# Attention levels copied under masks, pooling set between weight slots, norm statistics kept on VectorE

## Chip, cores and metric

The kernel runs on one core of one Trainium2 chip. The metric is the device time of one execution in microseconds. Before the change it is 1908.38 us (median of 3 runs, 1907.46 to 1908.57).

## What is computed

Two blocks on 256 tokens of width 2048, all in float32. Block one has two layers of sliding-window and latent attention and isn't touched. Block two has an even layer (gated linear attention beside a convolution) and an odd layer (pooling), each with a modulation and a layer norm. Cut to what the change touches:

```
# even layer, one head of 4, 256 wide, 256 tokens, forward and backward:
#   o_i = sum_j (q_i * exp(g_i - g_j)) . k_j v_j  + state term, g = cumulative log gate
# odd layer
h = (x * (1 + sc) + sh) @ w_in_o                  # 256 x 4096
xp, gate = split(h, 2)                            # 2048 each
for g, window in enumerate((2, 4, 8, 16)):        # 512 columns each, window over grid rows
    z_g = window_mean(xp_g) - xp_g
    z_g = z_g @ w_pool[g]                         # 512 x 512
y = (z * pool_scale * silu(gate)) @ w_out_o       # 2048 x 2048
# behind each layer
x = layer_norm(alpha * x + gt * y, ln_g, ln_b)    # mean and variance over 2048
```

## The kernel before

**Weight stream.** All large products run over a stream of 504 slots. A slot is a 128 x 1024 piece of weights (512 KB). SyncE loads it into a ring of four stages; ScalarE rounds it to the high part `wh` (L257, `split_hi`); VectorE subtracts to get the low part `wl` (L278, `split_lo`); TensorE does 12 products of 128x512 with it (L325 to L327) and then frees one of four split buffers (`split_free`). Eight slots make a group, that is 512 output columns, in one of two PSUM banks `L[0]`, `L[1]`; an evacuation frees the bank (`psum_free`). The input `xth`/`xtl` of a product is made by transposes (L404, two PSUM banks `TP`), rounded by ScalarE (L424) and subtracted by VectorE (L430). Every engine runs its own list in order; semaphores by name tie them. Between slots VectorE also sums up the modulation (`mod_next`, L569).

**Gated attention.** For each of four heads, pairs of tokens are treated in levels of block size b = 1, 2, ... 64, then 128 between the two halves, then the state term (level index v = 0 to 8). In a level ScalarE takes four exponentials (L881) of prefix and suffix sums, VectorE scales queries and keys with them (L1394, L1395), TensorE forms the products (L1936) into `AB[0]` or `AB[1]` in turn and then does one weight slot, and VectorE updates the sums for the next level (L1400 to L1403; the pair L1400/L1401 feeds the keys' side, L1402/L1403 the queries'), splits one slot (L278) and adds the previous level's products to the score matrix: `masked(v - 1)` multiplies the bank with the level's 0/1 mask into `LT` (L1385), waits, and adds `LT` to `ATd` (L1386); for level 7 it copies the bank to `ATo` (L1388). The masks of the levels don't overlap. At the head's end TensorE multiplies `ATd`, `ATo` and the states with the values (L1950 to L1954) into `AB[0]`. Ahead of the levels stand the head's transposes, its gate product (L1917), ScalarE's log-sigmoid (L905 to L908), VectorE's gate (L1363) and two fills with zeros (L1365, L1366).

**Odd layer.** 64 slots (`R_ODD`, eight groups: four of `xp`, four of `gate`), written as a first group with transposes, one group, and a loop over three pairs. ScalarE copies each group to `Z` or `gate`. Then TensorE does the four pooling sums (L1997), each waiting for VectorE's L1537 (`pooled`) of the one before, while ScalarE applies silu to all of `gate` (L1010). Then 8 pooling slots (`pool_step`) with transposes of `Z` between; `evac_pool` scales the result into `Z` (L1546) and multiplies with the gate (L1549). When all four are done (`y_done`), the transposes of `Z` and the 32 output slots follow, with the modulation of the gate rows (L1800) behind the first group, and `evac_residual` adds each group to `X` (L1481, L1486). ScalarE issues three row loads (L960) for that before it.

**Layer norm.** After the last residual ScalarE sums `X` (L975) and squares the deviations (L979), two passes of 2048 each; VectorE turns the sums into mean and variance (L1493, L490), ScalarE takes the root (L485, with a table load), VectorE the reciprocal and `nmr` (L493, L1496), ScalarE scales `X` (L987), VectorE applies gain and shift (L1505, L1506).

Of the kernel before, what the change touches and what calls it, by code (L numbers as in the profile page):

```python
# [19 lines left out]
P = 128  # L20
# [94 lines left out]
def build(nc, A, out):  # L115
    ctx = ExitStack()
    with ctx:
# [33 lines left out]
        st = sb("st", [P, 64])  # L151

# [94 lines left out]
        LT = pa[:, 1024:1280].rearrange("p (j i) -> p j i", j=TT)  # L247
# [352 lines left out]
        def _(act):  # L600
# [295 lines left out]
            for hd in range(GH):  # L896
# [16 lines left out]
                for v, b in enumerate(LEVELS + [128]):  # L913
                    k = 9 * hd + v
                    act.wait_ge(once("sums_ready"), k + 1)
                    if k:
                        act.wait_ge(once("qk_scaled"), k)
# [5 lines left out]
                    if (hd, v) in EVAC:  # L923
# [9 lines left out]
                                     AB[0][:, :].rearrange("p (t n) -> p t n", t=TT), ACT.Copy)\  # L933
# [36 lines left out]
            def layer_norm_act(k, e):  # L970

                act.wait_ge(psum_free, (G_BLOCK1 + R_KV + R_EVEN + R_OUT + k * (R_ODD + 4 + R_OUT)) + 2)
                junk = [ar(0, D), ar(6144, D)]
                for t in range(TT):
                    ins = nc.scalar.activation(junk[t], X[:, t, :], ACT.Copy, accum_out=ss[:, t:t + 1])  # L975
                ins.then_inc(once("ln_sum"), 1)
                act.wait_ge(once("ln_mu"), k + 1)
                for t in range(TT):
                    ins = nc.scalar.activation(junk[t], X[:, t, :], ACT.Square, bias=nmu[:, t:t + 1],  # L979
                                               accum_out=ss[:, t:t + 1])  # L980
                ins.then_inc(st_sum, 1)
                stats_act_root(act, rstd, e)
                act.wait_ge(once("ln_nmr"), k + 1)
                for c in range(4):
# [3 lines left out]
                    ins.then_inc(once("ln_scaled"), 1)  # L988

# [17 lines left out]
            split_pairs(act, split_hi, R_ODD0, 2, evac_to(0, 1024, 2048), turn=turn_odd)  # L1007
            split_pairs(act, split_hi, R_ODD0 + 4, 2, evac_to(4096, 1024, 2048))
            act.wait_ge(psum_free, G_BLOCK1 + R_KV + R_EVEN + R_OUT + R_ODD + 2)
            nc.scalar.activation(ar(4096, 4096), ar(4096, 4096), ACT.Silu).then_inc(once("gate_silu"), 1)  # L1010
            turn_and_split(act, split_hi, R_POOL0, turn_plain)
            act.wait_ge(once("y_done"), 2)
# [3 lines left out]
            split_pairs(act, split_hi, R_OUTO0, R_OUT // 2, None, final=True, turn=turn_plain)  # L1016
# [4 lines left out]
        def _(dve):  # L1021
# [330 lines left out]
            for hd in range(GH):  # L1352
# [6 lines left out]

                for d, dst in ((0, PF), (1, SB_)):  # L1360
# [180 lines left out]
            def evac_pool(g):  # L1541
# [8 lines left out]
                if g == 3:  # L1550
                    ins.then_inc(once("y_done"), 1)
# [12 lines left out]
            def turn_y1(m):  # L1564
                turn_plain(m)
                if m == SLOTS + 1:
                    gate_rows(1)
# [555 lines left out]
```

## Time and profile before

| | us |
|---|---|
| median of 3 runs | 1908.38 |
| the profiled execution's own time | 1907.66 |
| its span, first to last instruction | 1905.9 |
| TensorE products busy | 1771.0 (93%) |
| VectorE busy | 1333.5 (70%) |
| ScalarE busy | 939.7 (49%) |
| mean granted TensorE clock, share of full | 0.962 |

Busy time of products includes their overlap once. The span is what the profile shows; the time of an execution is 1.8 us longer here. A row of a timeline gives start and duration; an operation's duration may overlap the start of the next on the same engine by some 0.08 us, so steps are read from start to start. What stands in brackets is how long the engine was idle before and who released it. "issue" as releaser means that the profile shows none.

### The profile page before, as it was taken

The numbers are of one execution on the slowest core, as the hardware profiler recorded it, in microseconds if no ns is written. First come the engines' busy times: TensorE is split into PE (matmuls) and PEld (weight loads), VectorE is DVE, ScalarE is ACT, GpSimd is POOL, SyncE is SP. The second block draws the span as 40 slices with busy tenths as digits, with TensorE's granted clock in tenths as the row PEclk, the third lists the DMA queues.
The fourth block names the chain that finished last, engine by engine and source line by source line (L and its number), as shares of the span: only waits on it lengthen the run. The fifth ranks groups of instructions, "written<-read, shape, count | busy, mean of one in ns | idle before, by whom it ended". The sixth has DMA issues, their size and how long they took to land.

```text
span 1905.9 us, 22383 instructions
## 1 busy us (share of the span) xinstructions
PE 1771.0 (93%) x8116; PEld 1418.8 (74%) x8116; DVE 1333.5 (70%) x1777; ACT 939.7 (49%) x1389; POOL 139.2 (7%) x197
## 2 busy tenths in 40 slices
PE   6999999999999999999899989998989969998894
PEld 5887777878877778788577877776767758885683
DVE  4967777768677777678466688776876966664554
ACT  5546553455465634546554446555433374443334
POOL 1100000001000000011111100000100201110000
PEclk9999999999999999999799999999989979999997
DMA  8855444558654446689577733334965948882551
GB/s 274 289 195 188 164 152 154 177 173 284 216 187 155 156 149 231 214 314 321 177 230 247 275 113 119 116 111 142 333 253 189 349 162 285 290 290 86 188 179 64
DMA packets 107011, 390.30 MB, mean 205 GB/s; under 512 B 12407, under 2 KB 13183, under 8 KB 105215
## 3 DMA queue, kind: packets, MB, share of 16 engines
q1 hardware_dynamic: 75040, 268.99, 40.4%
q0 software_dynamic: 27648, 100.68, 16.9%
q10 hardware_dynamic: 4224, 19.31, 2.7%
q8 instruction: 62, 1.02, 0.2%
q14 instruction: 37, 0.30, 0.1%
HBM read 384.74 MB, written 4.19 MB: 204 GB/s over the span
## 4 chain that ended last, share of the span: by engine, by line
PE 79%; DVE 11%; ACT 4%; issue 3%; DMA 2%; ACTq 0%; SPq 0%; DVEq 0%
PE L L325 22%; PE L L327 21%; PE L L326 21%; PE TP L404 3%; DVE wl L278 2%; PE AB L1663 1%; DMA mstage<-in_w_mod 1%; PE AB L1592 1%; PE AB L1668 1%; PE AB L1997 1%; PE TP L1677 1%; PE AB L1667 1%; PE AB L1882 1%; PE AB L1954 1%; ACT wh L257 1%
## 5 line engine op out<-in xcount | busy, mean ns | idle before, releaser
L278 DVE TENSOR_TENSOR wl<-stage,wh 128x1024 fp32r<-128x1024 f32 x504 | 614.0, 1222 | 301.0 <-ACT wh L257 299.7
L325 PE MATMUL L<-wh,xth 128*128 128x512 f32 x1952 | 800.9, 410 | 11.2 <-issue 8.3
L257 ACT ACTIVATE wh<-stage 128x1024 fp32r<-128x1024 f32 x504 | 531.2, 1056 | 526.0 <-PE L L327 452.6
L327 PE MATMUL L<-wh,xtl 128*128 128x512 f32 x1952 | 774.6, 397 | 0.0
L326 PE MATMUL L<-wl,xth 128*128 128x512 f32 x1952 | 773.8, 396 | 0.0
L325 PEld LDWEIGHTS L<-wh,xth 128*128 128x128 f32 x1952 | 375.3, 192 | 104.2 <-issue 26.3
L327 PEld LDWEIGHTS L<-wh,xtl 128*128 128x128 f32 x1952 | 374.1, 192 | 82.3
L326 PEld LDWEIGHTS L<-wl,xth 128*128 128x128 f32 x1952 | 375.0, 192 | 76.5 <-issue 3.4
L569 DVE SCALAR_TENSOR_TENSOR macc<-mstage,scols,macc 128x1024 f32<-128x1024 f32 x240 | 307.1, 1279 | 11.4 <-DMA mstage<-in_w_mod 10.7
L593 POOL DMA_DIRECT2D mstage<-in_w_mod x192 | 138.8, 723 | 1568.0 <-DVE macc L569 966.0
L881 ACT ACTIVATE arena<-arena 128x256 f32<-128x256 f32 (+1 forms) x136 | 48.2, 425 | 63.9 <-DVE arena L1403 63.9
L679 ACT ACTIVATE pa<-TP 128x384 f32<-128x384 f32 x48 | 23.6, 491 | 105.7 <-PE TP L1677 105.7
L1103 DVE SCALAR_TENSOR_TENSOR pa<-tab,AB 128x384 f32<-128x384 f32 x48 | 26.6, 554 | 67.6 <-PE AB L1663 36.8
L667 ACT ACTIVATE pa<-pa,st 128x128 f32<-128x128 f32 x96 | 43.0, 450 | 56.1 <-DVE st L1112 36.4
L404 PE MATMUL TP<-ident,arena 128*128 128x128 f32 x344 | 52.9, 287 | 17.1 <-DVE xtl L430 7.6
L404 PEld LDWEIGHTS TP<-ident,arena 128*128 128x128 f32 x344 | 43.2, 149 | 28.3 <-issue 9.7
L404 PE MATMUL TP<-ident,X 128*128 128x128 f32 x144 | 24.5, 302 | 36.1 <-DVE X L1506 16.0
L404 PEld LDWEIGHTS TP<-ident,X 128*128 128x128 f32 x144 | 19.7, 156 | 40.4 <-issue 21.0
L424 ACT ACTIVATE xth<-TP 128x512 fp32r<-128x512 f32 x40 | 23.4, 590 | 52.3 <-PE TP L404 52.3
L643 ACT ACTIVATE arena<-L,st 128x512 f32<-128x512 f32 x60 | 37.8, 682 | 9.2 <-PE L L327 4.9
L430 DVE TENSOR_TENSOR xtl<-TP,xth 128x512 fp32r<-128x512 f32 x40 | 27.3, 686 | 14.5 <-ACT xth L424 14.5
L430 DVE TENSOR_TENSOR xtl<-pa,xth 128x512 fp32r<-128x512 f32 x40 | 27.6, 689 | 7.7 <-ACT xth L424 7.7
(184 smaller groups left out, 1380.8 us busy)
## 6 DMA issues: line engine op xcount, KB each, us to landing
stage<-in_w_stream SPq DMA_DIRECT2D x504, 512.0 KB, 4.4
mstage<-in_w_mod POOLq DMA_DIRECT2D x192, 512.0 KB, 6.3
X<-in_x SPq DMA_DIRECT2D x4, 512.0 KB, 8.5
arena<-in_ctx ACTq DMA_DIRECT2D x1, 2048.0 KB, 15.1
x_kept<-X ACTq DMA_DIRECT2D x1, 2048.0 KB, 10.1
X<-x_kept ACTq DMA_DIRECT2D x1, 2048.0 KB, 8.3
arena<-in_b_ada ACTq DMA_DIRECT2D x2, 1024.0 KB, 9.1
arena<-in_ln_b ACTq DMA_DIRECT2D x2, 1024.0 KB, 12.7
```

Of the source, the lines that this page charges most:

```text
L257: nc.scalar.activation(wh[:, s % SPLITS].rearrange("p a b -> p (a b)"), stage[:, s % RING, :], ACT.Copy).then_inc(hi_ready, 1)
L278: nc.vector.tensor_tensor(wl[:, s % SPLITS].rearrange("p a b -> p (a b)"), stage[:, s % RING, :], wh[:, s % SPLITS].rearrange("p a b -> p ...
L325: nc.tensor.matmul(o, xh, w[0], start=start, stop=False, skip_group_check=True)
L326: nc.tensor.matmul(o, xh, w[1], start=False, stop=False, skip_group_check=True)
L327: last = nc.tensor.matmul(o, xl, w[0], start=False, stop=True, skip_group_check=True)
L404: last = nc.tensor.transpose(bank[0:width, j, t * P:t * P + P], src(t), ident[:])
L430: nc.vector.tensor_tensor(lo, src[:, 0:n, :], hi.bitcast(F32), ALU.subtract).then_inc(bank_free(m), 1)
L569: nc.vector.scalar_tensor_tensor(out=acc, in0=block, scalar=col, in1=acc, op0=ALU.mult, op1=ALU.add).then_inc(mod_sum, 1)
L593: pool.dma_start(mstage[:, unit % MOD_UNITS, :].rearrange("p (c n) -> p c n", c=2), WM[n // KPB, :, 2 * cp:2 * cp + 2, COLS * k:COLS * k + ...
L643: ins = nc.scalar.activation(dst(t), L[bank][:, t, :], fn, scale=scale(t))
L667: ins = nc.scalar.activation(pr[b][:, a:a + w], pr[b][:, a:a + w], ACT.Exp, bias=ngm[:, 2 * b + t:2 * b + t + 1], scale=1.0 if swa else ML ...
L881: return nc.scalar.activation(dst, src, ACT.Exp, scale=1.0 / 16)
```

## The change

Four edits, all in block two:

1. `masked(v)` for levels 0 to 6 becomes one predicated copy of the product's bank into `ATd` under the level's mask, read as integers; `LT` goes. The last level (b = 128) leaves out L1400 and L1401 and the wait behind them. The final product waits for `ATo` only ahead of its last member, which moves behind the state products, and goes to `AB[1]`.
2. The two fills with zeros are issued ahead of the gate (L1363) and signal `sums_ready` there; ScalarE waits for the gate by itself in level 0.
3. The layer norm's mean and variance come from VectorE: `evac_residual` takes partial statistics (`bn_stats`) of each 512 columns, `layer_norm_dve` aggregates them; ScalarE's four passes go. `psum_free` is signalled with the first of the two residual additions.
4. In the odd layer every engine's list is written out slot by slot. ScalarE evacuates `gate` with silu directly. The pooling sums stand behind slots 33, 41, 49 and 53 of the 64, the transposes of `Z` behind the eight slots of the last group, and the transposes of the gated product behind pooling slots 3, 5, 7 and output slot 1; `y_done` is counted by group. The row loads wait for the last group.

```diff
-                        link(nc.vector.tensor_tensor(LT, bank, mk, ALU.mult))
-                        nc.vector.tensor_tensor(ATd, ATd, LT, ALU.add).then_inc(added, 1)
+                        nc.vector.copy_predicated(ATd, mk.to_broadcast([P, TT, P]), bank).then_inc(added, 1)
...
-                        nc.vector.tensor_tensor(sf[:, :, 0, :], sf[:, :, 0, :], pf[:, :, 1, b - 1:b].to_broadcast(shape), ALU.add)
-                        link(nc.vector.tensor_tensor(pb[:, :, 1, :], pb[:, :, 1, :], sb_[:, :, 0, 0:1].to_broadcast(shape), ALU.add))
+                        if b < P:
+                            nc.vector.tensor_tensor(sf[:, :, 0, :], sf[:, :, 0, :], pf[:, :, 1, b - 1:b].to_broadcast(shape), ALU.add)
+                            link(nc.vector.tensor_tensor(pb[:, :, 1, :], pb[:, :, 1, :], sb_[:, :, 0, 0:1].to_broadcast(shape), ALU.add))
...
+                nc.vector.memset(SF, 0.0)
+                nc.vector.memset(PB_, 0.0).then_inc(once("sums_ready"), 1)
                 for d, dst in ((0, PF), (1, SB_)):
...
-                nc.vector.memset(SF, 0.0)
-                nc.vector.memset(PB_, 0.0).then_inc(once("sums_ready"), 1)
...
-                pe.wait_ge(once("at_added"), k + 1)
+                pe.wait_ge(once("at_added"), k)
...
+                    if t == 0:
+                        pe.wait_ge(once("at_added"), k + 1)
+                    last = nc.tensor.matmul(o, ATo[:, 1 - t, :], Vf[:, 1 - t, vs], start=False, stop=True)
...
+                        if t == 0:
+                            ins.then_inc(psum_free, 1)
+                    link(ins)
+                    for t in range(TT):
+                        ins = nc.vector.bn_stats(parts[:, t, 2 * i + b, :], X[:, t, at(1024 * i + 512 * b, 512)])
+                    ins.then_inc(once("ln_parts"), 1)
...
             def layer_norm_dve(k, e):
+                dve.wait_ge(once("ln_parts"), 4 * k + 4)
+                for t in range(TT):
+                    ins = nc.vector.bn_aggr(moments[:, t, :], parts[:, t].rearrange("p g s -> p (g s)"))
+                link(ins)
+                mean, var = moments[:, :, 0], moments[:, :, 1]
+                nc.vector.tensor_scalar(rstd, var, 1.0, LN_EPS, ALU.mult, ALU.add).then_inc(st_ms, 1)
+                dve.wait_ge(st_sd, e + 1)
+                nc.vector.reciprocal(rstd, rstd).then_inc(st_rs, 1)
...
# ScalarE, odd layer
+            for n in range(4, 68):
+                if n < 10:
+                    turn_odd(n - 2)
+                hi()
+                if n >= 60:
+                    turn_plain(n - 60)
+                if n % 8 == 3 and n > 8:
+                    g = (n - 11) // 8
+                    slots_done(act, ODD + n - 3)
+                    for t in range(TT):
+                        dst = (Z if g < 4 else gate)[:, t, COLS * (g % 4):COLS * (g % 4) + COLS]
+                        ins = nc.scalar.activation(dst, L[g % 2][:, t, :], ACT.Copy if g < 4 else ACT.Silu)
+                    ins.then_inc(psum_free, 1)
+            hi(4)
+            for i in range(4):
+                if i:
+                    hi(2)
+                for m in range(2 * i, 2 * i + 2):
+                    turn_plain(m)
+            act.wait_ge(once("y_done"), 5)
...
# VectorE, odd layer
+            for n in range(4, 68):
+                if n < 10:
+                    turn_x1(n - 2)
+                lo()
+                mod_some(96, n - 4)
+                if n in (38, 46, 54, 58):
+                    pooled((38, 46, 54, 58).index(n))
+                if n >= 60:
+                    turn_plain(n - 60)
+            lo(2)
+            evac_pool(0)
+            lo(2)
+            evac_pool(1)
+            for i in range(4):
+                if i:
+                    lo(2)
+                if i in (1, 2):
+                    evac_pool(i + 1)
+                for m in range(2 * i, 2 * i + 2):
+                    turn_plain(m)
+            lo(5)
+            gate_rows(1)
...
# TensorE, odd layer
+            for n in range(SLOTS, 8 * SLOTS):
+                g, m = n // SLOTS, n % SLOTS
+                slot(pe, 8 * R_ODD0 + n, G + g, KPB * m, m == 0)
+                if n in (33, 41, 49, 53):
+                    pool_sums((33, 41, 49, 53).index(n))
+                if g == 7:
+                    pe.wait_ge(once("pooled"), m // 2 + 1)
+                    uses.append(turn_z(m))
...
+            for m in range(SLOTS):
+                turned(pe, uses[m])
+                slot(pe, 8 * R_POOL0 + m, G + R_ODD + m // 2, KPB * m, m % 2 == 0)
+                if m in (3, 5, 7):
+                    turn_y((m - 3) // 2)
+            for n in range(4 * SLOTS):
+                g, m = n // SLOTS, n % SLOTS
+                if n == 2:
+                    turn_y(3)
+                if g == 0:
+                    turned(pe, ys[m])
+                slot(pe, 8 * R_OUTO0 + n, G + R_ODD + 4 + g, KPB * m, m == 0)
+                if n == 7:
+                    modulation_gate(1)
```

## Rows read from the trace of the kernel before

**Rows 1.** Part 4 of the page: the chain that ended last, by engine.

```profile
PE 79%; DVE 11%; ACT 4%; issue 3%; DMA 2%; ACTq 0%; SPq 0%; DVEq 0%
```

**Rows 2.** Timeline of ScalarE, last slots (start, us, operation, [idle before]).

```profile
1865.14 1.06 ACT L257 ACTIVATE wh<-stage 128x1024 fp32r<-128x1024 f32 x1 [1.66 <-PE L L327]
1867.86 1.06 ACT L257 ACTIVATE wh<-stage 128x1024 fp32r<-128x1024 f32 x1 [1.66 <-PE L L327]
```

**Rows 3.** Busy time by stretch: one head, start of the pooling.

```profile
core 0: us, PE busy (x) PEld busy (x) DVE busy (x) ACT busy (x) POOL busy (x), PEclk, DMA share, GB/s
1145.43:1201.53 56.10, 51.09 (x258) 41.28 (x257) 45.57 (x85) 30.99 (x55) 0.00 (x0) 1.00 0.34 114
1719.00:1749.00 30.00, 21.99 (x63) 10.86 (x63) 10.78 (x15) 9.67 (x9) 0.00 (x0) 0.94 0.17 56
```

**Rows 4.** Timeline of VectorE, second head: level 1's start, level 6.

```profile
1162.11 0.69 DVE L1394 TENSOR_TENSOR pa<-arena 128x512 f32<-128x512 f32 x1 [0.44 <-ACT arena L881]
...
1185.11 0.68 DVE L1394 TENSOR_TENSOR arena<-arena 128x512 f32<-128x512 f32 x1
...
1186.31 0.42 DVE L1400 TENSOR_TENSOR arena<-arena 128x256 f32<-128x256 f32 x1
...
1187.44 0.42 DVE L1403 TENSOR_TENSOR arena<-arena 128x256 f32<-128x256 f32 x1
1187.78 1.22 DVE L278 TENSOR_TENSOR wl<-stage,wh 128x1024 fp32r<-128x1024 f32 x1
1188.91 0.42 DVE L1385 TENSOR_TENSOR pa<-AB,tab 128x256 f32<-128x256 f32 x1
...
1189.71 0.69 DVE L1394 TENSOR_TENSOR pa<-arena 128x512 f32<-128x512 f32 x1
```

**Rows 5.** Timeline of ScalarE there: exponentials of levels 1, 7 and 8.

```profile
1160.57 1.44 ACT L881 ACTIVATE arena<-arena 128x256 f32<-128x256 f32 x4 [1.22 <-DVE arena L1403]
...
1187.90 1.34 ACT L881 ACTIVATE arena<-arena 128x256 f32<-128x256 f32 x4 [2.31 <-DVE arena L1403]
...
1192.50 1.15 ACT L881 ACTIVATE arena<-arena 128x512 f32<-128x512 f32 x2 [2.31 <-DVE arena L1403]
```

**Rows 6.** Timeline of TensorE there: level 7, slot's last product, values.

```profile
1191.05 1.16 PE L1936 MATMUL AB<-pa 128*128 128x128 f32 x8 [0.68 <-DVE pa L1395]
...
1194.57 0.39 PE L327 MATMUL L<-wh,xtl 128*128 128x512 f32 x1
...
1196.08 0.67 PE L1950 MATMUL AB<-X,tail 128*128 128x256 f32 x2 [1.12 <-DVE tail L1388]
```

**Rows 7.** Timeline of VectorE around the first layer norm.

```profile
1523.02 1.29 DVE L1486 SCALAR_TENSOR_TENSOR X<-X,pa 128x512 f32<-128x512 f32 x2
...
1532.58 0.17 DVE L490 TENSOR_SCALAR st<-st 128x2 f32<-128x2 f32 x1 [4.14 <-ACT arena L979]
```

**Rows 8.** Timeline of ScalarE around the first layer norm.

```profile
1532.57 1.28 ACT L485 ACT_TABLE_LOAD   x1
...
1534.49 0.81 ACT L987 ACTIVATE X<-X,st 128x512 f32<-128x512 f32 x1 [0.43 <-DVE st L1496]
```

**Rows 9.** Groups of VectorE by line, first 900 us: the reduction.

```profile
L1107 DVE TENSOR_REDUCE st<-pa 128x1 f32<-128x256 f32 x48 | 19.6, 409 | 0.0
```

**Rows 10.** Timeline of TensorE from the last gate slot to the modulation.

```profile
1721.77 0.39 PE L327 MATMUL L<-wh,xtl 128*128 128x512 f32 x1
...
1797.61 0.60 PE L404 MATMUL TP<-ident,arena 128*128 128x128 f32 x4
...
1800.82 0.60 PE L404 MATMUL TP<-ident,arena 128*128 128x128 f32 x4
...
1809.45 3.00 PE L1800 MATMUL AB<-macc,ones 128*128 128x512 f32 x6
```

**Rows 11.** Timeline of TensorE, convolution's shifts: two sites, three slots between.

```profile
1366.93 1.88 PE L1971 MATMUL AB<-X,tab 128*128 128x512 f32 x4
...
1376.86 1.88 PE L1971 MATMUL AB<-X,tab 128*128 128x512 f32 x4
```

**Rows 12.** The row loads of L960 (six DMAs): time to landing.

```profile
DMA to landing us min/median/max: 6.5/9.8/14.3
```

More of the change, by code:

```diff
@@ L988, in layer_norm_act @@
                     ins.then_inc(once("ln_scaled"), 1)
+            Z, gate = ar(0, TT, D), ar(4096, TT, D)
             def turn_y(m):
@@ L1005, in turn_odd @@
                 turn_modulated(m, 2)
[L1007 to L1012, printed above, removed]
+            hi.n = 8 * R_ODD0 + 4
+            ODD, POOL, OUTO = 8 * R_ODD0, 8 * R_POOL0, 8 * R_OUTO0
+            for m in range(2):
+                turn_odd(m)
+            for n in range(4, 68):
[18 more added lines that the diff above has]
+            act.wait_ge(once("y_done"), 5)
             row_load(1, "b_ada", 4096)
@@ L1015, in _ @@
             row_load(1, "ln_b", 8192)
-            split_pairs(act, split_hi, R_OUTO0, R_OUT // 2, None, final=True, turn=turn_plain)
+            hi(OUTO + 4 * SLOTS - hi.n)
             layer_norm_act(1, 2 * DEPTH + 3)
@@ L1528, in turn_x1, with pooled @@
                 turn_scaled(m)
-            split_pairs(dve, split_lo, R_ODD0, 2, None, turn=turn_x1, beside=lambda i, n: mod_some(96 + 8 * i, n))
-            split_pairs(dve, split_lo, R_ODD0 + 4, 2, None, beside=lambda i, n: mod_some(112 + 8 * i, n))
+            lo.n = 8 * R_ODD0 + 4
             Z, gate = ar(0, TT, D), ar(4096, TT, D)
-            for g in range(4):
+            GO = G_BLOCK1 + R_KV + R_EVEN + R_OUT
+            def pooled(g):
                 dve.wait_ge(once("pool_sums"), g + 1)
@@ L1999, in _, with turn_z, turn_y @@
                 last.then_inc(once("pool_sums"), 1)
-            def pool_step(m):
-                g = m // 2
-                if m % 2 == 0:
-                    pe.wait_ge(psum_free, G + R_ODD + g + 1)
-                pe.wait_ge(lo_ready, 8 * R_POOL0 + m + 1)
-                for k in range(KPB):
-                    last = products(L[g % 2], m % SPLITS, k, KPB * m + k, m % 2 == 0 and k == 0)
-                last.then_inc(split_free, 1)
-            xt_pe(pe, u, Z, pool_step, lambda m: pe.wait_ge(once("pooled"), m // 2 + 1))
-            pe.wait_ge(once("y_done"), 2)
-            product_pairs(pe, R_OUTO0, G + R_ODD + 4, 2, turn=xt_group(pe, u, Z, R_OUTO0, G + R_ODD + 4),
-                          after=lambda: modulation_gate(1))
+            def turn_z(m):
+                transposes(pe, u, [lambda t, kt=2 * m + j: Z[:, t, kt * P:kt * P + P] for j in range(2)])
+                return u.n
+            xt_group(pe, u, X, R_ODD0, G, lambda m: pe.wait_ge(once("ln_done"), m // 2 + 1))()
+            uses = []
+            for n in range(SLOTS, 8 * SLOTS):
[6 more added lines that the diff above has]
+                    uses.append(turn_z(m))
+            ys = []
+            def turn_y(i):
+                pe.wait_ge(once("y_done"), i + 2)
+                for m in range(2 * i, 2 * i + 2):
+                    ys.append(turn_z(m))
+            for m in range(SLOTS):
[7 more added lines that the diff above has]
+                    turn_y(3)
+                if g == 0:
+                    turned(pe, ys[m])
+                slot(pe, 8 * R_OUTO0 + n, G + R_ODD + 4 + g, KPB * m, m == 0)
+                if n == 7:
+                    modulation_gate(1)
 def tables():
```

77 lines of the change are left out of this document (29 added, 48 removed).

## The prediction

> **What bounds the kernel now.** I read the chain of waits first. Four fifths of it are TensorE, a tenth VectorE [rows 1]: the kernel is a stream of 504 weight slots, and wherever the stream runs alone a slot costs TensorE 2.72 us (two splits by ScalarE, each released by the last product of a slot, lie 1867.86 - 1865.14 apart) [rows 2]. An edit off that path is worth nothing, so I looked for the stretches in which TensorE does not run slots back to back, with the view of busy time by stretch, and then at the timelines of the engines there. The change touches three such places. (a) The four heads of the gated attention: TensorE is busy 51.1 of 56.1 us of a head, and VectorE 45.6 [rows 3]. (b) The pooling: TensorE is busy 22 of 30 us from 1719, and much of that is pooling sums and not slots. (c) Two layer norms, in which TensorE stands still.
>
> **Part 1, levels under masks (four heads).** The reader is to see in VectorE's timeline that it has no idle time in a level: from one scaling (L1394) to the next are 4.60 us (1185.11 to 1189.71), of which the masked product and the addition (L1385, L1386) take 0.80 (1188.91 to 1189.71), the split L278 1.13, and the scalings and prefix sums 2.67 [rows 4]. The change makes one predicated copy of the two operations and of the wait between them. The trace has no predicated copy. The nearest row is L1400, an operation on 256 elements like it, 0.42 us; back to back such an operation costs 0.34 (L1403 to L278). I take 0.34, because one input comes from PSUM and one is the mask, as in L1385. The least is 0.2 (the 0.42 less what a start overlaps); the most I put at 0.61, a second pass over its 256 elements: L1394 with 512 elements takes 0.26 more than L1400 with 256.
>
> VectorE alone would then need 4.60 - 0.80 + 0.34 = 4.14. But another wait is close behind. The exponentials of the next level wait for the prefix sums and the next scaling for them: L1403 ends 2.75 after the first scaling (1187.86 - 1185.11), ScalarE starts 0.04 later and takes 1.34 [rows 4, 5]. In level 0, where nothing is masked, the scaling starts 0.10 after the exponentials' end (1160.57 + 1.44 = 1162.01, scaling at 1162.11, after 0.44 of idle time). So the level becomes 2.75 + 0.04 + 1.34 + 0.10 = 4.23 and the gain is 0.37, not 0.46. Any copy under 0.43 gives the same. TensorE needs about 3.7 us for a level: its products start at 1191.05 and the last product of the slot behind them is issued at 1194.57 and 0.23 long [rows 6], so it isn't the bound. Six of the intervals of a head (level 1 to 2 up to 6 to 7) gain it: 2.2 us.
>
> The last level drops two sums and the wait between them. Three steps take 1.13 (L1400 at 1186.31 to L1403 at 1187.44), and the one that stays 0.34, so 0.79 go [rows 4]; its exponentials are two, 1.15 us [rows 5]. VectorE would be 0.46 + 0.79 = 1.25 earlier at the final scaling, and the product with the values no longer waits for the copy L1388, but only for the scaling. Here TensorE itself is late next: level 7's products start 1.34 after the scaling of that level, its slot ends at about 1194.78, that is 3.73 later, so the values can start 5.07 after it instead of 6.37 (1196.08 - 1189.71) [rows 4, 6]. That is worth 1.3, not the 1.25 + 0.4 that the two edits promise apart. A head gains 2.2 + 1.3 = 3.5, four heads **14.0 us**.
>
> Zeros ahead of the gate: two fills leave the place between the gate's logarithm and the splits. ScalarE reaches the exponentials of level 0 only after its own second split of the head and a table load, so I count nothing (bounds -0.2 and +0.2 a head, that is the two sides of one operation of 256 elements).
>
> **Part 2, norm statistics (twice).** Before, after the last residual (L1486, ends 1523.02 + 1.29 = 1524.31) ScalarE makes two passes of copies and two of squares, loads a table at 1532.57 for 1.28, and starts to scale at 1534.49: 10.18 us [rows 7, 8]. After, VectorE has kept partial statistics at each of the four evacuations, and only those of the last lie on the path. For a statistic over 512 elements the nearest row is the reduction of 256, 0.409 [rows 9]; with the 0.26 for 256 more it is 0.67, 0.6 back to back. Chain: wait 0.04, two statistics 1.28, column update, two aggregations (tiny, like L490's 0.17) with their waits 0.45, epsilon 0.2; the table load starts (1532.57) before L490, the tiny operation that feeds the root, does (1532.58), so the wait doesn't hold it and it slides under the last slots; root, reciprocal and the product take what they take now, 0.64 (1533.85 to 1534.49). Sum 2.6; gain 10.18 - 2.6 = **7.6 us**, twice 15.2. Bounds of one statistic: 0.3 (half of what the reduction's row gives) to 1.2 (two passes), so 0.6 more to 1.2 less gain a norm; if the load is held by the wait, 1.3 is lost a norm. The six other pairs of statistics (1.3 us each) lie beside slots, where VectorE has a split of 1.13 and at most one multiply-add of similar length in 2.72; the split buffer is four deep, so a delay of 1.3 is not seen by TensorE. If that cover failed, it would be 6 x 1.3 = 7.8.
>
> **Part 3, pooling between slots.** Before, from the last slot's last product (1721.77 + 0.23 = 1722.0) to the start of the gate's modulation (L1800, 1809.45) are 87.4 us [rows 10]. In it: the pooling sums in a row with VectorE after each, a 4096-wide activation, 8 pooling slots, the wait for the last gated product, 8 output slots. After, the same TensorE work without the waits:
> - four groups of sums of four 128x512 products each, set between slots of the second half. Two such products (L1971) between slots stretch three slots from 8.16 to 9.93 (1366.93 to 1376.86) [rows 11], so 1.77 for two, 3.54 for four, 14.2 in all;
> - 8 transposes of Z behind slots: a slot with one takes 3.21 (1797.61 to 1800.82) [rows 10], 0.49 more, 3.9 in all;
> - 8 pooling and 8 output slots, 16 x 2.72 = 43.5;
> - 8 transposes of the gated product, 3.9 at the same price (they come in pairs and should cost a little less).
> Sum 65.5; gain 87.4 - 65.5 = **21.9 us**.
>
> Whether the waits go, I worked out slot by slot with these durations, counted from the first pooling slot. The pooled rows have slots between: sums 0 behind slot 33, VectorE takes them behind split 38, and sums 1 come behind slot 41. The third pooling bank needs VectorE's first evacuation (two operations of 512, one of 1024: 1.3 and 1.13 us, as in rows 4) by 10.9 + 0.85 us; it has read the bank at 9.1. The gated products end at 10.3, 15.8, 22.1, 28.5, and TensorE asks at 10.9, 17.2, 23.5, 29.8. Transposes of a pair also need the two banks of the pair before, freed at about 17.0, 23.4 and 29.8: nothing to spare. I count no stall, with 0 to 3 us in the range. The three rows for the final norm are issued at about 33 and needed at 47; such rows take up to 14.3 us to land [rows 12], so this too is just in time. No DMA is moved ahead of the weight queue. The activation goes into the evacuations from PSUM, and its table load under a slot. The loops over three pairs of groups are written out; as the slots of block one, also written out, I price that at nothing.
>
> **Sum.** 14.0 + 15.2 + 21.9 = 51.1. The profiled execution took 1907.66 (span 1905.9), so 1856.6; the median shown, 1908.38, is 0.7 above it: 1857.3, and I predict 1857.
>
> A page that speaks against part 1: the Trainium skill, VectorE: DVE Perf Modes, section "First, the fixed hardware budget", has two read ports a lane as the ceiling for the tensors that an instruction reads in a cycle. A predicated copy that fetched its old destination too would read three. By that rule the time would be that of rival 1 without the statistics, 1861; by L1385's row, where two inputs run in one pass, it is the forecast [rows 4]. The trace of before has no instruction with three.
>
> **Rivals.**
> 1. *Second pass.* Predicated copy at 0.61: the level is VectorE's, 3.80 + 0.61 = 4.41, gain 0.19 in six intervals, 1.3 at the end as before: 2.4 a head, 9.8 in all, 4.2 less. Statistics at 1.2 take another 1.2 x 2. 1857 + 6.6 = 1863.6. For: beside mask and new values the old ones have to stay, which may be done by reading them. Against: L1385 does as much with its operands in one pass. 0.13.
> 2. *The pooling's waits move instead of going.* VectorE is late with a gated product or with banks, or the rows land late and hold the modulation; the slack was zero in three places, and where TensorE waits for some us, as it does for each sum now, its clock falls too (granted 0.94 from 1719 to 1749) [rows 3]. The middle is a third of the gain, 7: 1864, up to 1872. For: the zero slack. Against: ScalarE and VectorE have only 1.1 and 1.7 us of work for a slot. 0.10.
> 3. *Slower than before.* The predicated copy as an operation that goes element by element, with 28 of them in VectorE's loop and everything behind them late. Norms, pooling, the dropped sums (4 x 0.79) and the freed copy L1388 (4 x 0.4) bring 41.9, so it decides from 41.9 / 28 = 1.5 us above the present 0.80, at 2.3 us a copy; at 3 us it is 28 x 2.2 - 41.9 = 20 slower, 1928. Nothing in the rows is near that (0.42 for 256 elements of any kind). 0.02.
> 4. *The heads don't gain*, since their end is set by another wait and what a level saves returns as a wait there: 1857 + 9 = 1866. Against: VectorE has no idle time in a level. 0.03.
>
> **Numbers.** Forecast 1857 with 0.72 (its own spread 1854 to 1860). The range 1853 to 1865 adds rival 1 and half of rival 2. What this measurement can tell from no change is about 0.2%, 4 us; all but rival 3 lie far beyond it: faster 0.97, same 0.01, slower 0.02.
>
> **What would show it.** Scalings 4.23 apart in levels 1 to 6, with VectorE idle 0.1 before them and ScalarE's exponentials as releaser; the predicated copy 0.42; first product with the values 5.1 behind level 7's scaling; ScalarE's scaling 2.6 behind the last residual, no table load between; slots 2.72 or 3.21 apart from the gates to the modulation, sums 3.5 between them, full clock throughout. Wrong it would be, if TensorE's timeline has gaps over 1 us there, or if a table load stands behind the statistics.

## Result and profile after

| | before | after |
|---|---|---|
| median, us (range, executions) | 1907.92 (1902.51 to 1908.57, 4) | 1851.46 (1847.59 to 1855.12, 4) |
| ratio of the executions | | 0.971, interval 0.9682 to 0.9738 |
| profiled execution, its own time / span | 1907.66 / 1905.9 | 1855.12 / 1853.3 |
| mean granted TensorE clock | 0.962 | 0.969 |

The kernel is 2.9% faster. The four executions before are the three named above and one beside the changed kernel (1902.51). The profiled execution lies 1.5 us from the 1856.6 of the prediction's sum; the median of the four, 1851.46, lies below its range (1853 to 1865). Both have to be explained, and they are two different things.

Page, part 4, the chain that ended last, by engine [rows 1]:

```profile
PE 81%; DVE 10%; ACT 4%; issue 2%; DMA 1%; SPq 0%; ACTq 0%; DVEq 0%
```

Timeline of VectorE in the second head, the scalings of levels 5 to 8 and the copies before them [rows 4]; L1398 is the predicated copy, L1406 the scaling:

```profile
1173.00 0.44 DVE L1398 COPY_PREDICATED tail<-tab,AB 128x256 f32<-128x256 uint32 x1
1173.43 0.69 DVE L1406 TENSOR_TENSOR pa<-arena 128x512 f32<-128x512 f32 x1
...
1177.24 0.44 DVE L1398 COPY_PREDICATED tail<-tab,AB 128x256 f32<-128x256 uint32 x1
1177.67 0.69 DVE L1406 TENSOR_TENSOR arena<-arena 128x512 f32<-128x512 f32 x1
...
1181.91 0.69 DVE L1406 TENSOR_TENSOR pa<-arena 128x512 f32<-128x512 f32 x1
...
1184.92 0.44 DVE L1398 COPY_PREDICATED tail<-tab,AB 128x256 f32<-128x256 uint32 x1
1185.25 0.68 DVE L1406 TENSOR_TENSOR arena<-arena 128x512 f32<-128x512 f32 x1
```

Timeline of ScalarE there, the exponentials [rows 5], and of TensorE, level 7 and the values [rows 6]:

```profile
1176.23 1.34 ACT L882 ACTIVATE arena<-arena 128x256 f32<-128x256 f32 x4 [1.95 <-DVE arena L1416]
```

```profile
1183.26 1.16 PE L1976 MATMUL AB<-pa 128*128 128x128 f32 x8 [0.32 <-DVE pa L1407]
...
1187.02 0.59 PE L1990 MATMUL AB<-X,tail 128*128 128x256 f32 x2
```

The scalings are 4.24 apart (1181.91 - 1177.67), 4.60 before. The step from the copy to the scaling is 0.43 where the exponentials end late (1176.23 + 1.34 = 1177.57), and 0.33 at the end of the head (1184.92 to 1185.25), where they are done: that is the copy's own step. The values start 5.11 behind level 7's scaling, 6.37 before, and TensorE no longer waits for them.

Timelines of VectorE, then of ScalarE, around the first norm [rows 7, 8]:

```profile
1506.42 1.22 DVE L279 TENSOR_TENSOR wl<-stage,wh 128x1024 fp32r<-128x1024 f32 x1
1507.56 1.28 DVE L1494 TENSOR_TENSOR pa<-L,arena 128x512 f32<-128x512 f32 x2
1508.87 1.29 DVE L1499 SCALAR_TENSOR_TENSOR X<-X,pa 128x512 f32<-128x512 f32 x2
1510.20 1.29 DVE L1505 BATCH_NORM_STATS2 parts<-X 128x6 f32<-128x512 f32 x2
...
1511.52 0.39 DVE L1512 BATCH_NORM_AGGREGATE moments<-parts 128x2 f32<-128x24 f32 x2
1511.94 0.17 DVE L1515 TENSOR_SCALAR st<-moments 128x2 f32<-128x2 f32 x1
```

```profile
1503.32 1.06 ACT L258 ACTIVATE wh<-stage 128x1024 fp32r<-128x1024 f32 x1 [0.76 <-PE L L328]
1504.39 1.28 ACT L486 ACT_TABLE_LOAD   x1
1512.14 0.20 ACT L486 ACTIVATE st<-st 128x2 f32<-128x2 f32 x1 [6.47 <-DVE st L1515]
1512.78 0.81 ACT L980 ACTIVATE X<-X,st 128x512 f32<-128x512 f32 x1 [0.43 <-DVE st L1519]
```

From the end of the last residual (1508.87 + 1.29 = 1510.16) to the scaling are 2.62 us, 10.18 before. The table load is issued ahead of the wait for the statistics, directly behind the last split.

Busy time by stretch (columns as in [rows 3]): one head, and the last 68.6 us up to the gate rows' modulation:

```profile
1139.93:1192.50 52.57, 50.70 (x258) 41.47 (x257) 42.55 (x76) 30.98 (x56) 0.00 (x0) 1.00 0.36 122
1696.00:1764.60 68.60, 68.60 (x333) 57.06 (x332) 51.68 (x55) 31.82 (x40) 0.72 (x1) 1.00 0.65 231
```

In the second row TensorE is busy for 68.60 of 68.60 us at full clock; in the kernel before it was busy 22 of 30 at the start of the pooling. Not one of the old waits has come back.

To say where the time went, I cut each trace at five points that every kernel has: the first product of a head with the values, the modulation of the gate rows, the start of the last residual group, ScalarE's first scaling of the norm, and again the gate rows. Differences of starts in us (heads: the mean period; even output: gate rows to last residual; odd: scaling to gate rows):

| | head | even output | residual to scaling | odd | last output | its residual to scaling |
|---|---|---|---|---|---|---|
| before | 56.10 | 71.51 | 12.79 | 274.96 | 69.23 | 12.80 |
| after | 52.59 | 73.52 | 5.22 | 251.70 | 69.22 | 5.23 |

The span is 52.5 us shorter. Of this, four heads bring 14.0, the odd layer 23.3 and the norms 15.1; the even output groups give back 2.0, and 2.0 come from ahead of the first line that differs. That adds up to 52.4.

### The profile page after: what moved, and what is told of

Same layout as the page of the kernel before. It is cut to its first block, busy times and chain, and to the rows that moved or that the text cites. A ratio compares the mean times of both kernels' runs of the same rounds, so it can differ in the third digit from the quotient of the medians.

```text
span 1853.3 us, 22300 instructions
## 1 busy us (share of the span) xinstructions
PE 1761.7 (95%) x8116; PEld 1415.7 (76%) x8116; DVE 1329.8 (72%) x1759; ACT 919.4 (50%) x1372; POOL 139.2 (8%) x197
## 4 chain that ended last, share of the span: by engine, by line
PE 81%; DVE 10%; ACT 4%; issue 2%; DMA 1%; SPq 0%; ACTq 0%; DVEq 0%
PE L L326 22%; PE L L328 22%; PE L L327 22%; PE TP L405 3%; DVE wl L279 2%; PE AB L1703 1%; PE AB L1632 1%; DMA stage<-in_w_stream 1%; PE AB L1708 1%; DVE macc L570 1%; PE TP L1717 1%; PE AB L1707 1%; ACT wh L258 1%; PE AB L1993 1%; PE AB L1922 1%
## 5 line engine op out<-in xcount | busy, mean ns | idle before, releaser
L431 DVE TENSOR_TENSOR xtl<-TP,xth 128x512 fp32r<-128x512 f32 x40 | 27.0, 685 | 10.4 <-ACT xth L425 10.4
L431 DVE TENSOR_TENSOR xtl<-pa,xth 128x512 fp32r<-128x512 f32 x40 | 27.6, 689 | 7.5 <-ACT xth L425 7.5
```

The costliest lines, as they stand in the source:

```text
L431: nc.vector.tensor_tensor(lo, src[:, 0:n, :], hi.bitcast(F32), ALU.subtract).then_inc(bank_free(m), 1)
```

## Experiments

**The changed kernel again, and each part alone.** The first run is the changed kernel unedited; the others are the kernel before with edits 1 and 2, with edit 3, and with edit 4.

> The changed kernel once more, the same code. The traces of before and after differ by 52.55 us of span, of which 1.97 lie ahead of the first line that the change touches, and the four executions of after spread over 7.5 us. Theory A (the terms were right, 51 to 52 us, and what moved the median out of the range is a spread of the whole program that has nothing to do with the change): against the kernel before on the same chip the gain is 50.5 to 52.5 us in the median, both kernels spread by several us, and the profile shows a different granted clock in stretches of block one. Theory B (the change gains more than its terms, 55 to 57 us, and the profiled execution was an unlucky one): gain 54 to 58 us, spread only in block two.

> Only the levels: predicated copy, dropped sums, freed last copy, fills ahead of the gate. By my terms 14.0 us less than before (3.5 a head, the level 4.24 us from scaling to scaling). Rival (the level was only paced by VectorE's 0.46 us): 18 us. Rival (something behind the heads gives it back): under 10 us.

> Only the norm statistics on VectorE. By my terms 15.2 us less than before, 7.6 a norm. In the trace of after the groups ahead of the first norm took 2.0 us longer than before; if the statistics between slots cause that (VectorE late with the modulation, so its loads are late), this kernel shows it too and gains 13 us, with TensorE waiting over 3 us for the last multiply-add of the modulation. If it is only how fast the loads came in that execution, it gains 15 us and the wait is as before, 1.3 us.

> Only the pooling between slots. By my terms 21.9 us less than before; the trace of after gives 23.0 between the first norm and the modulation, so 22 to 23. Rival (it needs the norm's shorter gap to come out so): 20 or less. No gap of TensorE over 1 us from the first gate group to the modulation.

| | median (range, executions) | ratio, interval | head | even output | residual to scaling | odd |
|---|---|---|---|---|---|---|
| again | 1854.70 (1848.91 to 1857.94, 5) | 0.9743, 0.9724 to 0.9761 | 52.56 | 73.17 | 5.22 | 251.88 |
| edits 1, 2 | 1890.62 (1888.35 to 1895.20, 6) | 0.9937, 0.9920 to 0.9953 | 52.58 | 72.10 | 12.79 | 274.55 |
| edit 3 | 1893.85 (1885.19 to 1897.25, 7) | 0.9954, 0.9935 to 0.9973 | 56.12 | 73.79 | 5.22 | 274.19 |
| edit 4 | 1879.00 (1877.24 to 1885.92, 4) | 0.9872, 0.9854 to 0.9890 | 56.11 | 71.82 | 12.79 | 252.18 |

The kernel before had 1902.67 beside them (1899.56 to 1908.24, 12). The heads are moved by edits 1 and 2 alone, the odd stretch by edit 4, the way from the residual to the scaling by edit 3, each by as much as in the changed kernel, so the stretches show no exchange between the parts. One column gets worse, the even output, and only where edit 3 is in. TensorE shows it too: ahead of the norm it waits for the last multiply-add of the modulation, for 3.62 us with edit 3 alone and for 1.29 before, as the expectation had it for that cause.

By the times the parts agree less well. Against the 1902.67 the medians gain 12.0 us (edits 1, 2), 8.8 (edit 3), 23.7 (edit 4) and 48.0 (all four); the intervals of the ratios make that 9 to 15, 5 to 12, 21 to 28, and 46 to 53. Edit 3 misses its 13 us: the trace has 15.1 less 2.0, which lies just above what the times allow. Only one of its seven executions was profiled, so why the others gained less isn't shown. All four together miss both theories in the median. Theory A's 50.5 to 52.5 lies in the interval, theory B's 54 to 58 doesn't. The kernel before alone spreads by 8.7 us here, in twelve executions on one chip, and the traces show such a spread in block one (the last experiment), which theory B didn't have.

**What the statistics cost beside the slots.** Statistics of three groups taken twice:

```diff
                     ins.then_inc(once("ln_parts"), 1)
+                    if k == 0 and 2 * i + b < 3:
+                        for t in range(TT):
+                            nc.vector.bn_stats(st[:, 52 + 6 * t:58 + 6 * t], X[:, t, at(1024 * i + 512 * b, 512)])
```

> The changed kernel with the partial statistics of the first three residual groups of the first norm taken twice (the second results are used by nothing): 3 x 1.3 us more for VectorE beside slots. If the 1.7 us that the even output groups gained with statistics is VectorE's lateness passed on to the last residual: the stretch from the gate rows' modulation to the last residual goes from 73.3 to 75 to 77 us. If VectorE's work beside slots is covered, as I forecast for it, and the 1.7 us are scatter or the weight transfers: it stays within 0.5 us of 73.3. The time: +2 to +4 us by the first, 0 by the second.

And the order of VectorE's last steps changed, with nothing left out (`lo` is a split, `mod_next` a modulation multiply-add, `evac_e` a residual group):

```diff
-            split_pairs(dve, split_lo, R_OUTE0, R_OUT // 2, evac_residual(0), turn=turn_y, beside=mod_oute)
-            mod_columns(dve, 7, 8, False, [(1, 2, 1)])
+            evac_e = evac_residual(0)
+            split_pairs(dve, split_lo, R_OUTE0, 1, evac_e, turn=turn_y, beside=mod_oute)
+            lo.n = 8 * R_OUTE0 + 2 * SLOTS + 4
+            for n in range(15):
+                if n == 8:
+                    group_done(dve, R_OUTE0 + 2)
+                    evac_e(1, 0)
+                lo()
+                if n < 14:
+                    mod_oute(1, n)
+            group_done(dve, R_OUTE0 + 3)
+            evac_e(1, 1)
             layer_norm_dve(0, 2 * DEPTH + 2)
+            mod_next(95)
             norm_columns(0, 0, 2048)
...
+                if m == 0:
+                    lo()
+                if m == 2:
+                    mod_columns(dve, 7, 8, False, [(1, 2, 1)])
```

> The changed kernel, with VectorE's last steps in the even layer's output groups put in another order: the last modulation multiply-add and the last split move behind the norm's mean and rstd, and the last modulation columns behind the first turns of the next layer, so that the last residual addition starts when TensorE's last product of the even layer ends instead of 4.3 us behind it. My theory (statistics make VectorE late by what the last residual waits for): from the gate rows' modulation to the last residual 73.5 becomes 69.5 to 70.5 us, nothing comes back behind, the whole 3 to 4 us shorter than the changed kernel, ratio to before 0.971 against 0.973. Rival (what is moved behind is missed there, by the modulated input or by the norm): the stretch is shorter by as much and the stretch from ScalarE's first scaling to the next gate modulation, 251.7 now, longer by 2 to 4 us; ratio as of the changed kernel. Second rival (the weight transfers set the stretch, DMA 0.93 to 0.96 busy in it): it stays at 73.5.

Taking it twice gave 1858.12 us (1852.56 to 1861.85, 4), ratio 0.976 (0.9733 to 0.9787); the interval overlaps those of the changed kernel, so its cost is read from the trace. The reordered kernel gave 1848.58 (1843.79 to 1849.65, 5), ratio 0.970 (0.9676 to 0.9724), the kernel before 1905.59 beside both (9). The even output groups, cut once more where TensorE's last weight product there is done (its start and the 0.23 us that a product costs in the stream):

| | TensorE, gate rows to its last product | from there to the last residual |
|---|---|---|
| before; edits 1, 2; edit 4 | 69.02; 69.00; 69.02 | 2.49; 3.10; 2.80 |
| after; again; edit 3 | 69.02; 69.02; 69.02 | 4.50; 4.15; 4.77 |
| statistics twice | 70.86 | 6.16 |
| reordered | 69.02 | 0.62 |

So the cover that I had named holds for TensorE's stream, which takes 69.02 us with and without statistics. But the last residual waits for VectorE itself, which carries a part of its lateness to the end. VectorE has a split and often a multiply-add in each slot there, and the multiply-adds also wait for their transfers. Timeline of VectorE in the changed kernel:

```profile
1501.30 1.28 DVE L570 SCALAR_TENSOR_TENSOR macc<-mstage,scols,macc 128x1024 f32<-128x1024 f32 x1 [0.52 <-DMA mstage<-in_w_mod]
1502.59 1.23 DVE L279 TENSOR_TENSOR wl<-stage,wh 128x1024 fp32r<-128x1024 f32 x1
1505.22 1.28 DVE L570 SCALAR_TENSOR_TENSOR macc<-mstage,scols,macc 128x1024 f32<-128x1024 f32 x1 [1.40 <-DMA mstage<-in_w_mod]
```

The wait of 1.40, the 1.20 of the multiply-add and one more split of 1.14 (1506.42, shown above) stand ahead of the last residual. With three more pairs (3.9 us) the residual comes 3.5 later (77.02 against 73.52, at the top of the 75 to 77 expected), and TensorE too is late by 1.8: nearly nothing is covered any more. Reordered, VectorE's timeline reads:

```profile
1497.87 1.22 DVE L279 TENSOR_TENSOR wl<-stage,wh 128x1024 fp32r<-128x1024 f32 x1
1499.01 1.28 DVE L1494 TENSOR_TENSOR pa<-L,arena 128x512 f32<-128x512 f32 x2
...
1504.12 1.28 DVE L570 SCALAR_TENSOR_TENSOR macc<-mstage,scols,macc 128x1024 f32<-128x1024 f32 x1
1505.78 1.23 DVE L1529 TENSOR_TENSOR X<-X,arena 128x1024 f32<-128x1024 f32 x1 [0.38 <-ACT X L980]
```

The multiply-add now lies in the time in which VectorE used to wait for the first scaled columns. The two operations that moved are 2.3 of the 3.9 us gained in this stretch; most of the rest is the wait of 1.40 for the transfer, which is gone too. The even output is 69.64 instead of 73.52, the odd layer 252.04 instead of 251.70 and 251.88: all but 0.3 us of the 3.9 stays. Both rivals fall. In this stretch the kernel is shorter than the changed one and than the one before (71.51). Its median is 2.9 and 6.1 us below the two of the changed kernel (1851.46 and 1854.70), about what the trace says, but by the times alone the intervals overlap; the 3.6 rest on one profiled execution.

**What sets a level.**

```diff
-                        nc.vector.copy_predicated(ATd, mk.to_broadcast([P, TT, P]), bank).then_inc(added, 1)
+                        nc.vector.copy_predicated(ATd[:, :, 0:1], mk.to_broadcast([P, TT, P])[:, :, 0:1], bank[:, :, 0:1]).then_inc(added, 1)
```

> The changed kernel with the predicated copy of levels 0 to 6 cut to one column of each half (the rest of the levels' products is left out). If ScalarE's exponentials set the level, as I forecast for every copy under 0.43 us: scalings stay 4.23 to 4.24 us apart, with VectorE's idle time ahead of them grown by what the copy loses (about 0.3 us). If VectorE's own instructions set it: 4.24 - 0.33 = 3.9 us apart, a head shorter by 2.0 us, and 8 us over four heads.

Timeline of VectorE:

```profile
1162.41 0.15 DVE L1398 COPY_PREDICATED tail<-tab,AB 128x2 f32<-128x2 uint32 x1
1162.83 0.69 DVE L1406 TENSOR_TENSOR arena<-arena 128x512 f32<-128x512 f32 x1 [0.27 <-ACT arena L882]
...
1166.64 0.16 DVE L1398 COPY_PREDICATED tail<-tab,AB 128x2 f32<-128x2 uint32 x1
1167.06 0.69 DVE L1406 TENSOR_TENSOR pa<-arena 128x512 f32<-128x512 f32 x1 [0.27 <-ACT arena L882]
```

The copy falls from 0.44 to 0.15, and the scalings stay 4.23 apart: what the copy loses appears as idle time ahead of the scaling, released by the exponentials. A head takes 52.50, against 52.59; the one execution took 1846.99 us. The level is set by the loop of prefix sums, exponentials and scaling, and a cheaper copy would shorten none.

**Fills and the wait for `ATo` undone.**

```diff
-                nc.vector.memset(SF, 0.0)
-                nc.vector.memset(PB_, 0.0).then_inc(once("sums_ready"), 1)
                 for d, dst in ((0, PF), (1, SB_)):
...
+                nc.vector.memset(SF, 0.0)
+                nc.vector.memset(PB_, 0.0).then_inc(once("sums_ready"), 1)
...
-                pe.wait_ge(once("at_added"), k)
+                pe.wait_ge(once("at_added"), k + 1)
```

> The changed kernel with two small edits taken back: the two zero fills stand behind the gate again, and the final product of a head waits for the copy into ATo ahead of its first member. Mine: the fills were hidden behind ScalarE, which comes to level 0 late anyway, and the copy ends long before TensorE is there, so a head stays at 52.6 us, at most 0.1 more. If each edit was worth its own instructions: 0.5 to 1.0 more a head for the fills and 0.4 for the copy.

The one execution took 1857.35 us. A head takes 52.66, 0.07 more than 52.59: both edits together are worth 0.3 us in four heads, which is hardly more than the 52.54 to 52.60 of the other traces with edits 1 and 2. In the changed kernel VectorE waits 0.92 us for level 0's exponentials, so it had time for the fills. The copy into `ATo` begins at 1186.46 and takes 0.42, so it ends 0.14 before the values start at 1187.02. I had given the two edits of the end 1.3 together and not 1.65, since TensorE is late next; the wait wasn't tried alone.

**How much slack the pooling has.** One, and two, extra products of 1024 elements ahead of each gated product:

```diff
+                nc.vector.tensor_tensor(pa[:, 0:1024].rearrange("p (t n) -> p t n", t=TT), Z[:, :, cs], gate[:, :, cs], ALU.mult)
                 nc.vector.tensor_tensor(Z[:, :, cs], Z[:, :, cs], gate[:, :, cs], ALU.mult).then_inc(once("y_done"), 1)
```

> The changed kernel with one more multiplication of 1024 elements (1.14 us, its result is used by nothing) ahead of each of VectorE's four gated products of the pooling. In the trace of the changed kernel the first gated product ends 0.40 us before TensorE's transposes of it (1727.81 and 1728.21), the others 1.3 us before them, and VectorE has 0.35 us of idle time in a period of 6.37. If nothing but this slack covers the waits: one stall of 0.75 us at the first, then at most 0.8 a period once the 1.3 are used up, so that the stretch from ScalarE's first scaling to the gate rows' modulation, 251.8 us, becomes 252.5 to 253.5. Rival (four buffers of splits and two banks cover more than my count by slots): 251.8 stays. Second rival (each wait comes back whole): 4 x 1.14, 256.4.

> The same with two such multiplications ahead of each gated product, 2.28 us. By the slack of the trace: a stall of 1.9 at the first, 0.7 at the second and 1.3 to 2 at each of the last two, since VectorE then has 8.3 us of work in a period of 6.4: 251.8 becomes 256 to 258.5, and TensorE's granted clock falls below 1.00 in the pooling. Rival (buffers cover it): under 253.

Timelines of TensorE, the transposes of the gated product, with one and then with two:

```profile
1726.08 1.09 PE L405 MATMUL TP<-ident,arena 128*128 128x128 f32 x8 [0.63 <-DVE arena L1579]
...
1739.69 1.16 PE L405 MATMUL TP<-ident,arena 128*128 128x128 f32 x8 [0.42 <-DVE xtl L431]
...
1746.76 1.16 PE L405 MATMUL TP<-ident,arena 128*128 128x128 f32 x8 [0.41 <-DVE xtl L431]
```

```profile
1727.69 1.09 PE L405 MATMUL TP<-ident,arena 128*128 128x128 f32 x8 [1.76 <-DVE arena L1580]
...
1743.58 1.16 PE L405 MATMUL TP<-ident,arena 128*128 128x128 f32 x8 [1.56 <-DVE xtl L431]
...
1751.77 1.16 PE L405 MATMUL TP<-ident,arena 128*128 128x128 f32 x8 [1.57 <-DVE xtl L431]
```

The executions took 1854.74 and 1859.78 us, and the odd stretch 255.29 and 258.45. The first stall is as expected (0.63 and 1.76 for 0.75 and 1.9). From the first transposes to the gate rows it was 36.27 in the changed kernel (1728.21 to 1764.48) and 38.03 and 41.45 here, so the pooling lost 0.63 + 1.76 = 2.4 us for one product and 1.76 + 5.18 = 6.9 for two; the rest of the 255.29 (1.2) arose ahead of it, in a stretch that these edits don't touch. With two the result is at the edge of what I expected, with one it is outside, and the pooling alone would be too. With one I had expected up to 1.7: the later pairs wait for the bank of transposes that VectorE's L431 frees, and not for the gated product, whose slack of 1.3 I had counted. I also expected the clock to fall with two; it stayed at 1.00 (third column from the end), by the view of busy time:

```profile
1690.00:1730.00 40.00, 38.24 (x188) 31.41 (x187) 31.68 (x34) 20.24 (x27) 1.45 (x2) 1.00 0.57 185
1730.00:1765.00 35.00, 30.76 (x145) 24.70 (x144) 29.26 (x32) 12.96 (x15) 0.00 (x0) 1.00 0.58 217
```

My prediction had read the 0.94 from 1719 to 1749 [rows 3] as what the wait before each sum costs. A narrower look at the kernel before doesn't bear this out. The waits before the second to fourth sum are 1.50 us each, and the clock between them is 1.00:

```profile
1731.23 3.70 PE L1997 MATMUL AB<-arena 128*128 128x512 f32 x8 [1.50 <-DVE arena L1537]
1736.43 3.70 PE L1997 MATMUL AB<-arena 128*128 128x512 f32 x8 [1.50 <-DVE arena L1537]
```

```profile
1730.00:1745.00 15.00, 10.76 (x24) 4.45 (x25) 3.99 (x6) 0.00 (x0) 0.00 (x0) 1.00 0.00 0
```

The low clock of that row lies at the first sum, which starts at 1724.33 behind a wait of 2.18 us and takes 5.40 where the others take 3.70.

So the waits are gone, but by a margin of 0.40 us at the first group and less than one operation of VectorE a period: rival 2 was near.

**Where the executions differ.** Nothing was edited for this; each trace above has block one, which is the same code in all. Busy time in two stretches of it, the kernel before and then the reordered one:

```profile
280.00:300.00 20.00, 19.13 (x90) 14.66 (x90) 13.85 (x22) 6.26 (x13) 0.72 (x1) 0.91 0.42 134
...
660.00:680.00 20.00, 19.13 (x90) 14.67 (x89) 12.88 (x21) 7.05 (x15) 0.73 (x1) 0.91 0.47 157
```

```profile
280.00:300.00 20.00, 19.13 (x97) 14.82 (x96) 15.29 (x25) 6.26 (x13) 0.72 (x1) 1.00 0.48 158
...
660.00:680.00 20.00, 19.12 (x98) 14.77 (x96) 15.28 (x26) 6.26 (x13) 0.73 (x1) 1.00 0.48 158
```

The third column from the end is the granted clock: at 0.91 a part of the stretch ran at 1.2 GHz instead of 2.4, at 1.00 none did. The code there is the same in both. Added up over stretches of 10 us, TensorE was at the low level for 68 us ahead of 1130 in five executions (before; again; edits 1, 2; edit 4; fills undone), for 65 in the profiled one of the changed kernel, for 58 in two (edit 3; two extra products) and for 55 in four. The first product with the values, with 3.5 added where the first head is shorter by edits 1 and 2, comes at 1139.8 to 1141.0 in the five, at 1138.0, at 1133.7 and 1135.2, and at 1131.6 to 1133.2 in the four. That is up to 9.4 us between executions before anything of the change has run, more in the executions with more low clock. The clock isn't all of it: 13 to 14 us more at half speed are some 7 us of products, and the means of the two groups lie 8.1 apart (1140.4 and 1132.2). Which clock an execution gets, and where the rest comes from, isn't settled here.

For the four executions of the result only the mean granted clock is on record, and it orders them as the times do: 0.969 at 1855.12, 0.971 at 1852.96, 0.973 at 1849.96, 0.974 at 1847.59. Where in the three unprofiled ones the low clock lay isn't shown. But the changed kernel's second profiled execution, with 68 us of low clock in block one like the profile of before, took 1857.94, within 1 us of the prediction.

## Why the prediction was right and wrong

- **Levels, 14.0.** Measured 4 x 3.52 = 14.1. The scalings are 4.24 apart (4.23), set by the exponentials, as the cut copy shows; the values come 5.11 behind (5.07); the copy's step is 0.33 (0.34). The two read ports of a lane (the Trainium skill, VectorE: DVE Perf Modes, section "First, the fixed hardware budget") would have meant rival 1 only if the old destination were read as a third tensor. A copy of 256 elements takes 0.44 and an addition of as many 0.42 (L1416), so nothing of a third tensor is to be seen, and rival 1 falls. Nor did the fills gain, as I had counted.
- **Norms, 15.2.** Measured 2 x 7.57 = 15.1. Chain 2.62 (2.6), a pair of statistics 1.29 (1.28), the table load under the slots, where I had put it on the ground that it starts before its input is there.
- **The six other pairs, 0.** Here a term was mis-sized: it costs 2.0 us, the mean of 73.2 to 74.9 in seven executions with single statistics (73.85) less that of 71.5 to 72.1 in three without (71.81). I had asked only whether TensorE sees VectorE late. Its stream doesn't; but the last residual is VectorE's own work, and there about half of the 3.9 us that three pairs add comes out. The last layer, in which no multiply-adds stand beside the slots, shows none of it (69.22, before 69.23). With the doubled statistics the cover fails for nearly all that is added (3.5 of 3.9), so in this layer my price for a cover that fails was of the right size.
- **Pooling, 21.9.** Measured 22.6: the odd stretch is 274.57 on average without the edit and 251.93 with it (3 and 7 executions, the two slowed on purpose left out; 251.3 to 252.7). A sum costs 3.43 (3.54), a slot with one transpose 3.21, a pair of transposes 0.93 (0.98); the cheaper sums and pairs make 0.6 of the 0.7 us above my term. The three places with no slack held; the gated product is ready 0.40 ahead (0.6).
- **Sum.** 14.1 + 15.1 - 2.0 + 22.6 = 49.8, for 51.1.
- **The median: the step that failed.** It reads "the median shown, 1908.38, is 0.7 above it: 1857.3, and I predict 1857", with a spread of its own of 1854 to 1860. I took three executions within 1.1 us for the kernel's level and spread. Over all 26 executions of it (4 of the result, 12, 9 and 1 beside the experiments, on at least three chips) it ran from 1899.56 to 1910.73 (mean 1904.4), and nine of the changed kernel from 1847.59 to 1857.94 (median 1854.2, mean 1853.2). The profile I worked from is one with 68 us at low clock in block one, the slow end; a sum that starts there gives the time of such an execution, and two came at 1857.94 (again) and 1857.35 (fills undone). The means differ by 51.3 us (48.8 to 53.8 by resampling), so the size of the change was right, and the level from which it was taken off was some 4 us too high. No step about the change itself explains a median below 1853: the terms as measured add up to 1.3 less than forecast, which goes the other way. The size of the miss is in part luck: the medians of the result differ by 56.5 us, those of the repetition by 48.0, where the changed kernel's median of 1854.70 would have been in the range.
- **Rivals.** Second pass: a step of 0.33 from one start to the next, not 0.61. Waits that move: none at the measured load, but three of four are back with one more operation a group, and all with two. What I said with it, that the clock falls as TensorE waits before each sum, was a misreading of a mean over 30 us. Slower: a copy costs a fifth of the price from which it decides. Heads: they gain in full.

## What to carry to other kernels

When work is put beside a stream, ask of each engine, not only of the one that bounds, who takes over at the end of the stretch: lateness that four buffers hide from TensorE can come out at the first step that is the late engine's own (2.0 of 3.9 us here, 3.5 of the next 3.9). Order the last steps of such an engine so that nothing unneeded stands ahead of that handover; this brought 3.6 us here, more than the 2.0 that the statistics had cost. And take the level and the range of a median from how much unchanged code varies between executions, not from the scatter of three times.

## What the runs showed of the hardware

- A predicated copy of 128 x 256 fp32 values from PSUM under an integer mask: 0.44 us, 0.33 to the next start.
- Partial statistics over 512 columns: two in 1.29 us. Aggregation of four such parts: two in 0.39.
- The same instructions at the same place are granted a different clock in different executions: 0.91 or 1.00 from 280 to 300 us. In sum TensorE's low level lasts 55 to 68 us of block one, and the same point behind it comes up to 9.4 us later in the executions with more of it; by its length the clock accounts for some 7 of them.
- Stalls of 1.1 to 1.8 us some 8 us apart (two extra products) did not lower the granted clock, which stayed at 1.00 from 1690 to 1765; nor did waits of 1.50 us every 5.2 us in the kernel before (1.00 from 1730 to 1745).
- A table load was done ahead of the wait of the operation that needs it: load at 1504.39, operation at 1512.14 behind 6.47 us of idle time.
